# Three blocks of a small language model in fp32: both ends of the kernel reordered, and four spots between them

## What is computed

```python
# block 1 (all sums over the tokens' features)
h = rms_norm(x, norm_mix);  u_pool, u_lru, q, k, v, g = split(h @ w_in)
x = x + (sum of gated branches: pooling, RG-LRU, stick-breaking attention) @ w_out
h2 = rms_norm(x, norm_ffn); x = x + (silu(h2 @ w_gate) * (h2 @ w_up)) @ w_down
# block 2
z, xbc, dt, q, k, v = split(rms_norm(x) @ ev_w_in)
y_a = rms_norm(ssd_chunked_scan(silu(conv(xbc)), dt) * silu(z), gate_norm)    # 16 heads
y_b = rms_norm((softmax(q1 k1) - lam * softmax(q2 k2)) v)   # differential attention, rope on q, k
x = x + concat(y_a, y_b) @ ev_w_out;  x = x + swiglu(rms_norm(x))
# block 3
x = x + concat(s5(...), mla(...)) @ od_w_out;  x = x + swiglu(rms_norm(x))
return rms_norm(x, norm_final)
```

## Time and profile before

| | before |
|---|---|
| runs | 2520.43, 2521.75, 2522.57 us |
| median | 2521.75 us |
| profiled execution | 2520.07 us |
| its span (first to last instruction) | 2518.3 us |
| mean granted clock of PE | 0.990 |
| PE, PEld | 2442.2 us (97%), 1962.8 us (78%) |
| DVE | 1301.7 us (52%) |
| POOL | 1059.2 us (42%) |
| ACT | 866.6 us (34%) |
| DMA | 213.58 MB, mean 85 GB/s |

### The profile page before, as it was taken

One profiled execution on the slowest core, in us unless ns is written; L12 is line 12 of the kernel. 1 busy time (PEld: TensorE's weight loads), 2 busy tenths in 40 slices (PEclk: granted clock), 3 DMA queues, 4 the chain that ended last, 5 costly groups with the idle time before them and its releaser, 6 DMA issues.

```text
span 2518.3 us, 30094 instructions
## 1 busy us (share of the span) xinstructions
PE 2442.2 (97%) x11662; PEld 1962.8 (78%) x11662; DVE 1301.7 (52%) x1928; ACT 866.6 (34%) x1360; POOL 1059.2 (42%) x830
## 2 busy tenths in 40 slices
PE   8999999999999999999999999999999889999998
PEld 6877767888888888876777778888888657788886
DVE  6336687533533321494767754686126855533301
ACT  4453346222322222334445533222224453322221
POOL 4323344644544444353322245554454223544442
PEclk9999999999999999999999999999999989999999
DMA  4212122232323233222222223323231112222232
GB/s 148 68 59 78 55 78 90 95 101 92 105 93 100 94 96 96 93 85 66 74 67 75 72 75 107 98 94 98 92 100 55 28 34 81 91 92 101 91 98 80
DMA packets 65646, 213.58 MB, mean 85 GB/s; under 512 B 7904, under 2 KB 10208, under 8 KB 65376
## 3 DMA queue, kind: packets, MB, share of 16 engines
q1 hardware_dynamic: 64496, 208.30, 25.8%
q10 hardware_dynamic: 1008, 3.35, 0.4%
HBM read 205.33 MB, written 2.10 MB: 82 GB/s over the span
## 4 chain that ended last, share of the span: by engine, by line
PE 88%; DVE 9%; issue 1%; ACT 1%; DMA 0%; DVEq 0%; ACTq 0%; SPq 0%
PE ps L632 25%; PE ps L633 24%; PE ps L634 24%; PE ps L653 1%; DVE T L2175 1%; PE ps L654 1%; PE ps L655 1%; PE ps L982 1%; PE ps L959 1%; PE ps L749 1%; PE ps L995 1%; PE ps L740 1%; PE ps L774 1%; PE ps L827 1%; DVE A L1893 0%
## 5 line engine op out<-in xcount | busy, mean ns | idle before, releaser
L603 POOL TENSOR_TENSOR w_lo<-w_raw,w_hi 128x512 fp32r<-128x512 f32 (+4 forms) x822 | 1049.5, 1301 | 1420.6 <-ACT w_hi L1302 1420.5
L632 PE MATMUL ps<-H,w_hi 128*128 128x512 f32 x1880 | 754.7, 401 | 21.3 <-DVEq L1870 11.4
L634 PE MATMUL ps<-H,w_lo 128*128 128x512 f32 x1880 | 736.8, 392 | 0.0
L633 PE MATMUL ps<-H,w_hi 128*128 128x512 f32 x1880 | 736.3, 392 | 0.0
L1302 ACT CAST w_hi<-w_raw 128x1024 fp32r<-128x1024 f32 (+4 forms) x411 | 402.9, 984 | 519.4 <-DMA w_raw<-in_weights_dram 513.1
L632 PEld LDWEIGHTS ps<-H,w_hi 128*128 128x128 f32 x1880 | 355.5, 189 | 115.2 <-issue 25.8
L632 PE MATMUL ps<-split,w_hi 128*128 128x512 f32 x1034 | 411.5, 398 | 6.8 <-issue 3.3
L634 PEld LDWEIGHTS ps<-H,w_lo 128*128 128x128 f32 x1880 | 355.1, 189 | 75.1
L633 PEld LDWEIGHTS ps<-H,w_hi 128*128 128x128 f32 x1880 | 355.6, 189 | 73.1 <-issue 2.7
L633 PE MATMUL ps<-split,w_hi 128*128 128x512 f32 x1034 | 403.4, 390 | 0.0
L634 PE MATMUL ps<-split,w_lo 128*128 128x512 f32 x1034 | 403.4, 390 | 0.0
(11 more groups left out here) (403 smaller groups left out, 2369.3 us busy)
## 6 DMA issues: line engine op xcount, KB each, us to landing
w_raw<-in_weights_dram SPq DMA_DIRECT2D x323, 512.0 KB, 3.5
w_raw<-in_weights_dram SPq DMA_DIRECT2D x48, 448.0 KB, 3.3
w_raw<-in_weights_dram SPq DMA_DIRECT2D x22, 256.0 KB, 2.6
A<-A SPq DMA_DIRECT2D x64, 64.0 KB, 2.0
X<-in_xt_dram SPq DMA_DIRECT2D x4, 512.0 KB, 7.9
out_dram<-A SPq DMA_DIRECT2D x8, 256.0 KB, 2.1
w_raw<-in_weights_dram SPq DMA_DIRECT2D x12, 128.0 KB, 2.0
w_raw<-in_weights_dram SPq DMA_DIRECT2D x6, 192.0 KB, 2.3
```

What stands on the lines that cost most here:

```text
L603: sub = nc.gpsimd.tensor_tensor(w_lo[:, p % NS, c], w_raw[:, p % NS, c], w_hi[:, p % NS, c].bitcast(F32), ALU.subtract)
L632: mm_(ps[:, bank, :], r(wh), xh, start=(k == 0), stop=False)
L633: mm_(ps[:, bank, :], r(wh), xl, start=False, stop=False)
L634: mm = mm_(ps[:, bank, :], r(wl), xh, start=False, stop=(k == kt - 1))
```

## The change

Both ends and four spots between are edited. No arithmetic is dropped; the last tile is computed in two halves of 256 tokens.

- Start: SP loads panel 2 before X tiles 4 to 7. ACT makes H[0] of each X tile (a copy with the gain as scale, `s_hhi`) and casts one panel after each pair; constants and masks are issued after the first pair, the squares come last. DVE makes only H[1]. PE runs four units of qk_a tiles 0 and 1 in turn, four of tile 2, then the rest of all three in turn.
- Rotary angles: `angle_parts`, four pieces, one behind times_dt of z tiles 1 to 4; the sines at t == 5, cosine and factors at t == 7. `BC_AT` runs products 4, 5 at z tile 6 and 6, 7 at tile 7.
- First maxima: `split_y(7)` behind `maxima(0)` and `maxima(1)`; `norm_cols("gate")` behind the fourth unit of dqk2's second tile.
- out2b's banks in the order 2, 3, 0, 1.
- out3b: H[0] on ACT as at the start, DVE adds, adds the square of the tile before, and makes H[1].
- End: down3's tile 7 in two halves in two banks, the first half's sums, root, spread and products beside the second half; products go to H and are stored as four DMAs per half, two tiles of 256 tokens each.

```diff
-    "out2a": (8, (8,), 128, (0, 1)), "out2b": (8, (8,), 128, (0, 1, 2, 3)),
+    "out2a": (8, (8,), 128, (0, 1)), "out2b": (8, (8,), 128, (2, 3, 0, 1)),
...
+        LAST_BANKS = (USE["down3", 7][0][0], 4)
+        SPREAD_BANKS = (7, 5)
...
-        _items.insert(1, (("cols", 0), 0))
+        _items[1:2] = [(("cols", 0), 4), (("rot", 8), 2)]
...
+        BC_AT = {2: (0,), 3: (1,), 4: (2,), 5: (3,), 6: (4, 5), 7: (6, 7)}
...
             x_part(1)
+            panel(2)
             x_part(2)
             x_part(3)
...
-            for k in range(KT):
-                sp.wait_ge(s_fin, k + 1)
-                sp.dma_start(out[P * k:P * k + P, :], area(S * k, S)).then_inc(s_out, 16)
+            for h in range(2):
+                c = slice(256 * h, 256 * h + 256)
+                for k in range(0, KT, 2):
+                    sp.wait_ge(s_fin, KT * h + k + 2)
+                    sp.dma_start(out[P * k:P * k + 2 * P, c].rearrange("(k p) s -> p k s", p=P), H32[:, 0, k:k + 2, c]
+                                 ).then_inc(s_out, 16)
...
+            def three_ahead(name, x, arrive):
+
+                a, b, c = [units((name, t), x, arrive) for t in range(3)]
+                for _ in range(4):
+                    next(a)
+                    next(b)
+                run(c, 4)
+                for _ in zip(a, b, c):
+                    pass
...
-            together("qk_a", (0, 1), HX, (s_h, H_BASE["mix"]))
+            three_ahead("qk_a", HX, (s_h, H_BASE["mix"]))
             pe.wait_ge(s_con, 16)
-            for t in range(2, 8):
+            for t in range(3, 8):
...
-                    products_bc(t - 2)
-            products_bc(6)
-            products_bc(7)
+                    for c in BC_AT[t]:
+                        products_bc(c)
...
-                    yield from units((f"dqk{p}", n), HX)
-                    if p == 2 and n == 0:
-                        norm_cols("gate", 7)
+                    for u, _ in enumerate(units((f"dqk{p}", n), HX)):
+                        if p == 2 and n == 1 and u == 3:
+                            norm_cols("gate", 7)
+                        yield
...
-            norm_cols("final")
-            norm_spread("final")
...
+            (_, use), = USE["down3", 7]
+            pe.wait_ge(bank_free[LAST_BANKS[0]], use)
+            for h in range(2):
+                c, o = slice(256 * h, 256 * h + 256), LAST_BANKS[h]
+                for p, k0, n in PARTS["down3", 7]:
+                    pe.wait_ge(w_ready[p % NS], p // NS + 1)
+                    for k in range(k0, k0 + n):
+                        if h == 1 and k == 9:
+                            final_cols(0)
+                        if h == 1 and k == 15:
+                            final_spread(0)
...
+            final_cols(1)
+            final_spread(1)
...
-            hi_to(2)
-            act.dma_start(C_[:], consts).then_inc(s_con, 16)
-            act.dma_start(MASKS32, masks).then_inc(s_msk, 16)
+            hi_to(1)
+            act.wait_ge(s_vec, 16)
+            for i in range(4):
+                act.wait_ge(s_xin[i], 16)
+                for k in (2 * i, 2 * i + 1):
+                    A_(HX[0](k), X[:, k, :], ACT.Copy, scale=vec("norm_mix", k)).then_inc(s_hhi, 1)
+                hi_to(i + 2)
+                if i == 0:
+                    act.dma_start(C_[:], consts).then_inc(s_con, 16)
+                    act.dma_start(MASKS32, masks).then_inc(s_msk, 16)
             for k in range(KT):
-                act.wait_ge(s_xin[k // 2], 16)
                 square("mix", k, X[:, k, :])
...
-                if t == 3:
+                if t == 5:
                     act.wait_ge(s_ang, 1)
...
-            x_squares("out3b", "ffn3")
+            for t in range(8):
+                hi_to(last_panel("out3b", t) + 4)
+                act.wait_ge(s_x, X_BASE["out3b"] + t + 1)
+                A_(HX[0](t), X[:, t, :], ACT.Copy, scale=vec("norm_ffn_2", 8 + t)).then_inc(s_hhi, 1)
+                square("ffn3", t, X[:, t, :])
...
-                scaled(HX, k, X[:, k, :], vec("norm_mix", k), s_h)
+                dve.wait_ge(s_hhi, k + 1)
+                link(v.scalar_tensor_tensor(HX[1](k), X[:, k, :], vec("norm_mix", k), HX[0](k).bitcast(F32),
+                                            ALU.mult, ALU.subtract))
+                dve.sem_inc(s_h, 1)
...
-                if t == 1:
-                    angles(POS, con("freq64"), ANG, ANG2, 16)
-                    dve.sem_inc(s_ang, 1)
                 times_dt(t)
-                if t == 5:
+                if 1 <= t <= 4:
+                    run(angle, 1)
+                if t == 7:
                     dve.wait_ge(s_sin, 1)
...
-            split_y(7)
...
             maxima(0)
             maxima(1)
+            split_y(7)
...
-            add_to_x("out3b", "ffn3", lambda k: ("norm_ffn_2", 8 + k))
+            for t in range(8):
+                done("out3b", t)
+                bank = bank_of("out3b", t)
+                link(v.tensor_tensor(X[:, t, :], X[:, t, :], ps[:, bank, :], ALU.add))
+                dve.sem_inc(bank_free[bank], 1)
+                dve.sem_inc(s_x, 1)
+                if t >= 2:
+                    add_square("ffn3", t - 1)
+                dve.wait_ge(s_hhi, KT + t + 1)
+                link(v.scalar_tensor_tensor(HX[1](t), X[:, t, :], vec("norm_ffn_2", 8 + t), HX[0](t).bitcast(F32),
+                                            ALU.mult, ALU.subtract))
+                dve.sem_inc(s_h, 1)
+            add_square("ffn3", 7)
...
+            dve.wait_ge(s_fhalf, 1)
+            last_x(0)
+            last_square(0)
+            final_rms(0)
+            products(0, range(0, 5))
+            done("down3", 7)
+            last_x(1)
+            products(0, range(5, 7))
+            last_square(1)
+            products(0, range(7, 8))
+            final_rms(1)
+            products(1, range(KT))
```

More of the change, by code:

```diff
@@ L519, in build @@
         s_fin, s_out = sem("final_ready"), sem("out_stored")
+        s_fhalf = sem("last_half_ready")
         block = ctx.enter_context(nc.Block())
@@ L584, in _ @@
             swap_at = {last_panel(f"dqk{p}", t) + NS: (p, t) for p in range(4) for t in range(4)}
-            for p in range(2, PANELS):
+            for p in range(3, PANELS):
                 if p in swap_at:
@@ L848, in ffn @@
                 tile(f"down{k}", 0, GU, (s_gu, FT * (k - 1)))
-                for t in range(1, 8):
+                for t in range(1, 7 if k == 3 else 8):
                     tile(f"down{k}", t, GU)
@@ L1325, in root, with x_squares @@
                 A_(ROOT, ps[:, bank, 0:4], ACT.Sqrt, bias=con("eps"), scale=1.0 / NORMS[NORM[n]][2]).then_inc(s_root, 1)
-            def x_squares(name, n):
-                for t in range(8):
+            def x_squares(name, n, tiles=8):
+                for t in range(tiles):
                     hi_to(last_panel(name, t) + 4)
@@ L1894, in scaled_out, with add_to_x @@
                 dve.sem_inc(bank_free[bank], 1)
-            def add_to_x(name, n, gain):
-                for t in range(8):
+            def add_to_x(name, n, gain, tiles=8):
+                for t in range(tiles):
                     done(name, t)
@@ L2148, in ffn @@
                         run(beside, 1 if j < FT - 1 else 1000)
-                add_to_x(f"down{k}", after, gain)
+                add_to_x(f"down{k}", after, gain, 7 if k == 3 else 8)
             at = VCOL["lambdas"][0]
@@ new lines, in _, with halves, last_x, last_square @@
+            add_square("ffn3", 7)
+            ffn(3, "final", None)
+            def halves(h):
+                return slice(256 * h, 256 * h + 256)
+            def last_x(h):
+                bank, c = LAST_BANKS[h], halves(h)
+                link(v.tensor_tensor(X[:, 7, c], X[:, 7, c], ps[:, bank, c], ALU.add))
+                dve.sem_inc(s_x, 1)
+            def last_square(h):
+                dve.wait_ge(s_sq, SQ_BASE["final"] + 7 + h + 1)
+                link(v.tensor_tensor(ACC[:, halves(h)], ACC[:, halves(h)], SQ[:, halves(h)], ALU.add))
+                dve.sem_inc(s_acc, 1)
@@ new lines, in final_rms, with products @@
+            def final_rms(h):
+                dve.wait_ge(s_root, NORM["final"] + h + 1)
+                link(v.reciprocal(RT[:, 2 * h:2 * h + 2], ROOT[:, 2 * h:2 * h + 2]))
+                dve.sem_inc(s_rt, 1)
+            def products(h, tiles):
+                dve.wait_ge(s_nspread, NORM["final"] + h + 1)
+                for k in tiles:
+                    v.scalar_tensor_tensor(H32[:, 0, k, halves(h)], X[:, k, halves(h)], vec("norm_final", k),
+                                           ps[:, SPREAD_BANKS[h], halves(h)], ALU.mult, ALU.mult).then_inc(s_fin, 1)
```

66 lines of the change are left out of this document (51 added, 15 removed).

## The result

| | before | after |
|---|---|---|
| median of 4 runs | 2521.09 us (2520.39 to 2522.57) | 2507.84 us (2507.24 to 2509.13) |
| profiled execution, its span | 2520.07, 2518.3 us | 2508.21, 2506.4 us |

The ratio is 0.9946, 95% interval 0.9934 to 0.9958. The change gains 13.2 us between the medians and 11.9 us between the two profiled executions; 20.2 were forecast. The time is 6.3 us above the predicted one. It lies 0.8 us outside the band of the forecast itself (2496 to 2507) and inside the wider range (2493 to 2511).

A forecast was written before the change was run, and what follows sets the result against it. PE, busy 97% of the span, bounds the kernel, so edits pay through its waits, half clock and ends. Seven terms sum to -20.2 us: 2520.07 to 2499.9, plus 1.7 to the median, said as 2501.5; range 2496 to 2507, wider 2493 to 2511.

The forecast's parts named there:

- Start: Kernel start: PE no longer runs out of H after its first wait; -2.4 us, ends -1.2 and -2.8.
- Rotary angles: z tiles: eight angle steps in four pieces remove PE's wait and half clock; 2.6 + 1.7 + 0.4 = -4.7 us.
- Products B and C: z's end: one ACT copy fewer, -0.7 us, offset by the moved product and late sine steps; 0.0, ends -0.8 and +1.5.
- First maxima: SSM's end to first transposes: maxima ahead of pair 7's split remove PE's wait and half clock; -6.3 us.
- Banks of out2b: out2b's start: banks 2 and 3 first remove PE's bank wait; -1.5 us, ends -0.9 and -1.7.
- Input of the third up: Before up3: ACT's cast comes 2.3 to 2.5 us earlier; -2.4 in waits, -1.7 for clock, together -4.1 us.
- Tail: Kernel's end: last tile in halves shortens what follows the last matmul; -1.2 us, ends -2.4 and +1.5.
- The first (only the nearer end is gained): At angles, maxima and up3 the next wait takes over; sum -9.6 to -11, about 2511 us; chance 0.15.
- The second (the clock falls elsewhere): Half clock appears at other places, 1.7 us per new fall; three more give 2506.5 us; chance 0.12.
- The third rival (SSM cold): SSM stage behind z, some 115 us, runs at 1.2 GHz; all of it gives 2558 us; chance 0.03.
- The fourth: Edits don't do what they say, waits having other causes; within 5 us of before, 2519 us; chance 0.04.
- the fifth: More is gained: up3's second wait goes and the tail reaches its better end; 2494 us; chance 0.06.

The follow-up runs named there:

- the kernel with 41.60 us: Kernel before with the start's edits alone, every other part as before: median 2519.03 us of 10 runs, ratio 0.9990.
- the second execution of before: Unchanged kernel before, run once more for a second trace: 2521.56 us.
- the kernel with the products undone: Changed kernel with three edits undone together (product order of B and C, out2b's banks, the tail in halves): 2511.02 us, one run.
- The repeat: Changed kernel run once more unchanged: median 2507.37 us, ratio 0.9943; its profiled execution took 2504.70 us.
- The two that put the cast first and also touch z's end: Changed kernel, out3b's cast ahead of ACT's square, plus sine steps at z tile 6 (2505.90 us) or ACT's last two z copies ahead of its cast (2505.41 us).
- the cast alone: Changed kernel with one line more: in out3b ACT casts the next panel before its square, behind its copy: 2506.35 us, ratio 0.9941.
- the kernel with the copies first: Changed kernel with out3b's cast ahead of ACT's square and, behind z tile 7, ACT's last two copies ahead of its cast: 2505.41 us, ratio 0.9947.

## Why the prediction was right, and where it was not

**What bounds the kernel.** Right: PE's busy share stayed at 97%, and the gains stand where waits went.

**Start.** -2.7 against -2.4; in the executions of the kernels with this start the stage takes 41.6 to 43.0 us, so -2.4 to -3.7. What differs is the clock: the first matmuls go from half clock's 0.63 us to 0.39 us each near 15.5 us in the kernel with 41.60 us, and near 18.3 us in the one with 42.97. No wait for H, as foreseen.

**Rotary angles.** -4.1 against -4.7, and 4.3 by the kernel with the angles in one piece. The terms 2.6 and 1.7 are right: 28.23 against the 25.63 us of the kernel with the products undone, and 29.93 against 28.23. The 0.4 for a turn and a product at half clock was counted twice, since both run inside the 3.4 us that the 1.7 pays for; and the product moved into this stage takes 0.2 back. That the 1.7 was there to be gained is luck of the execution: against the second execution of before the edit gives 2.4 us.

**Products B and C.** +0.4 against 0.0, inside the ends, for another reason than given. The order of the products gives -0.35 here (9.27 us, and 9.62 with it undone) and costs 0.18 in the stage before, so -0.2 where -0.4 was reckoned. The +0.4 charged for the late sine steps isn't there: with them late 9.62 us, with everything there as in before 9.61, both with 3.4 us at half clock. What is there is the clock, +0.7 against the 8.91 of before.

**First maxima.** -6.5 against -6.3, the best hit of a sum whose second half is luck: 3.2 us are the wait, always there, and 3.2 the clock, absent in one of three executions of before.

**Banks of out2b.** -1.3 against -1.5.

**Input of the third up.** The step that failed is "the cast comes 2.3 to 2.5 us earlier". DVE's round became shorter, 2.8 us to the fifth add (forecast 2.75), but the first two casts for up3 came only 0.5 and 0.1 us earlier. The prediction counted DVE's operations and left out ACT's queue, where copy, square and cast stand one behind the other and the square waits for DVE's sum of the tile before; this sum, said to lie "in the shadow", took up to 1.61 us beside POOL. With the cast moved ahead of the square it comes 2.3 and 2.7 us earlier, DVE's adds are 2.74 us apart up to the sixth, and the stage gains 3.6 us against before: the number was near for a kernel that was not the one to be timed. The waits fell by 0.1 us (3.79 to 3.65) instead of the 2.4 of the sum, where the rows of the prediction give 2.0 (1.49, and 2.30 less 1.75) and the rest has to be the restarts. The clock, expected to hold, fell for 6.8 us instead of the 3.4 of before. Together +0.6 instead of -4.1, which is 4.7 of the 8.3 us that are missing.

The longer fall is not the edit's alone: in the kernels with the angles whole and with three edits undone, whose code here is after's, it is 3.4 us and the stage takes 16.9 us. So at an equal fall the edit gives 0.1 us.

**Tail.** -1.35 against -1.2. The stores in 1 KB pieces landed in 2.2 us each, 2.1 before, so the bound in which they cost twice as much is refuted. The overhead of small transfers, of which the Trainium skill speaks in Perfetto Trace Analysis, DMA Optimizations, does not show here in 1 KB pieces of 256 KB stores.

**Rivals.** The first (only the nearer end is gained) happened at up3 only. Its total was mis-added: with 2.6, 3.2 and 1.1 at the three places the sum is -12.0, not -9.6 to -11. The second (the clock falls elsewhere) happened, and with it the prediction's own sign of being wrong, rows of 0.50 where there were none. The sum had taken 6.8 us of time for the clock as gained, and in the profiled executions the total at half clock stayed at some 41 us; 10.2 us stand behind the wait at 343 us, 3.4 behind z, 3.4 more at up3, and 6.8 fewer in the MLA.

In time the untouched stages cost 3.3 us (+3.8 and +1.6, the fall that moved from 257 to 284 us, and -2.1 in the MLA). With up3's 4.7 that is 8.0 of 8.3. Of the three, the first two come and go in executions of before as well, and so does the third: the MLA takes 129.0 to 129.2 us in three executions with the change's code and 131.1 to 132.6 in seven others. Behind z it is different. The clock falls there in all ten traces of kernels that have the change's z stage, in whole or in part, and in one of four with that of before, so that fall, 0.7 us, is better counted as a cost of the change; why it comes was not tried. The repeat, with some 31 us at half clock, gains 15.4 us of span.

The Trainium skill's TensorE: Matmul & The Clock Gate, Part 1, says that the monitor runs freely; equal waits of equal code that end at different clocks agree with it. The two waits that the prediction called equal were not (3.2 and 2.46 us); the repeats are what shows it.

The third rival (SSM cold) did not come: the SSM took 109.72 us for 109.75. With four other kernels it took 110.8 to 110.9, with 2.4 to 2.7 us at half clock. The fourth and the fifth did not come.

**A better kernel.** The two that put the cast first and also touch z's end have medians of 2505.4 and 2505.9 us, the cast alone 2506.35, after 2507.4 to 2507.8. The ranges overlap, the ratios to before do too, and the total expected of the cast alone, 2504 or less, was not reached. What is shown is the stage (13.44 for 17.60 us, in all three traces with both edits 13.4 to 13.5), not a faster total. The rest of its gain was taken back by half clock at other places in these traces (6.8 us at z's end, 23.9 in the MLA in each). Both places come before out3b, and the kernel with out3b as before shows the same 6.8 and 23.9 us, so this is no price of the cast. A total over more executions was not taken.

## What to carry to other kernels

When work moves from one engine to another, write down the receiving engine's whole queue, in order, with each step's own wait: an edit that shortens one engine's round can end behind a single buffer on the next. Two holds on the same step each hide the other's gain, so try both together before either is dropped. Count a wait as gained, and the clock behind it only in part: take the same wait in several executions of the unchanged kernel first.

## What the hardware showed that was not expected

A fall of the granted clock is not a property of the code alone. One wait of 3.22 us was followed by 10.2 us at 0.50, the same wait of 3.24 us by 1.00. In the runs of one kernel the time goes with the mean granted clock: the six of the kernel with the copies first run from 2502.86 us at 0.993 and 2502.73 at 0.992 over 2504.97 and 2505.85 at 0.991 to 2512.27 at 0.988 and 2515.57 at 0.986. A wait of 2.08 us at up3 was followed by full clock, two of 1.10 and 1.23 us by 6.8 us at half.

Very small DVE operations can pay as much as large ones while POOL works. The same step of one loop on 128 x 8 numbers in after, before POOL's stretch of four instructions and inside it:

```profile
34.01 0.17 DVE L1987 TENSOR_SCALAR small<-small 128x8 f32<-128x8 f32 x1
34.30 5.02 POOL L612 TENSOR_TENSOR w_lo<-w_raw,w_hi 128x512 fp32r<-128x512 f32 x4 [10.50 <-ACT w_hi L1357]
34.42 1.20 DVE L1987 TENSOR_SCALAR small<-small 128x8 f32<-128x8 f32 x1
```

0.17 us become 1.20, seven times as much, where 128 x 512 operations grow from 0.75 to 1.63 us. All four such steps inside POOL's stretch take 1.20 to 1.22 us, and their ends tell what they wait for: 35.62, 36.85, 38.10 and 39.34 us, each 0.02 to 0.03 us after one of POOL's four instructions ends (35.59, 36.83, 38.08, 39.32). The whole trace of after says the same: the 34 additions, products and copies of at most 16 columns that start inside a POOL instruction (0.06 us or more behind its start, 0.25 us or more before its end) all end within 0.06 us of its end. The eight reciprocals that start there don't wait; they take 0.17 to 0.18 us. So such a small step pays what is left of POOL's 1.3 us, whatever its own size. No run changed POOL's work to test this.
